# Low weight parts on GpSimd around hand-overs, and tiles that sweep the high weights first, in a two-layer streaming encoder

## What is computed

```python
def swiglu(x, w_gu, w_dn):
    gate, up = jnp.split(x @ w_gu, 2, axis=-1)
    return (jax.nn.silu(gate) * up) @ w_dn

def trunk_layer(...):
    x = x + 0.5 * rmsnorm(swiglu(rmsnorm(x, g[0]), w_gu0, w_dn0), g[1])
    u = rmsnorm(x, g[2])
    qa, ka, va, qb, kb, vb = jnp.split(u @ w_in, 6, axis=-1)
    ...
    mix = jnp.concatenate([oa, ob], axis=-1) @ w_out
    x = x + rmsnorm(mix, g[3])
    qc = rmsnorm(x, g[4]) @ w_cq
    oc = cross_attend(qc, mem_k, mem_v) @ w_co
    x = x + rmsnorm(oc, g[5])
    x = x + 0.5 * rmsnorm(swiglu(rmsnorm(x, g[6]), w_gu1, w_dn1), g[7])
```

## Time and profile before

| | |
|---|---|
| median of 3 runs | 2632.45 us (2627.0 to 2634.76) |
| the profiled execution's own time | 2635.67 us |
| its span, first to last instruction | 2633.9 us |
| PE busy | 2525.5 us, 96% |
| DVE, ACT, POOL busy | 1209.3, 912.3, 23.8 us |
| mean granted clock of PE | 0.982 |
| largest group of PE's waits | 19.7 us, for w_lo |

### The profile page before, as it was taken

The page is one execution under the profiler, slowest core; times in us unless marked ns, Lnnn a source line. Parts: engine busy times, 40 slices in busy tenths (PEclk is TensorE's granted clock), DMA queues, the critical chain, the costliest instruction groups (busy, mean ns, idle before and its releaser), DMA issues.

```text
span 2633.9 us, 47255 instructions
## 1 busy us (share of the span) xinstructions
PE 2525.5 (96%) x19325; PEld 2416.5 (92%) x19325; DVE 1209.3 (46%) x2059; ACT 912.3 (35%) x1650; POOL 23.8 (1%) x55
## 2 busy tenths in 40 slices
PE   6999999999999899999999999999999998999998
PEld 6999999997698799999989999989966988999998
DVE  4444325336747644442354442253466656444323
ACT  4222223225745522222232222242356545222221
POOL 1000000000000000000000000000000000000000
PEclk9999999999999999999999999999999998999999
DMA  6223333332123122232222223233411311322321
GB/s 185 87 85 89 95 88 102 98 114 91 39 83 105 36 85 88 88 99 81 77 64 88 88 88 99 85 97 115 125 55 49 115 47 50 94 87 84 94 87 66
DMA packets 384734, 229.81 MB, mean 87 GB/s; under 512 B 6892, under 2 KB 371454, under 8 KB 384608
## 3 DMA queue, kind: packets, MB, share of 16 engines
q1 hardware_dynamic: 379040, 206.66, 26.4%
q0 software_dynamic: 4368, 16.92, 1.9%
q10 hardware_dynamic: 1200, 4.46, 0.4%
HBM read 214.46 MB, written 18.79 MB: 89 GB/s over the span
## 4 chain that ended last, share of the span: by engine, by line
PE 88%; DVE 7%; ACT 2%; issue 1%; DMA 1%; DVEq 0%; ACTq 0%; SPq 0%
PE psum L671 75%; PE psum L646 4%; PE psum L959 3%; PE psum L727 2%; PE psum L991 2%; DVE w_lo L1495 1%; DVE x L1533 1%; PE psum L686 1%; ACT w_hi L1164 1%; DVE u_lo L1490 1%; PE psum L973 1%; DVE y_mix L1530 1%; DMA w_raw<-in_w_ffn_gu 0%; DMA w_raw<-in_w_cq 0%; DVE y_ffn L1530 0%
## 5 line engine op out<-in xcount | busy, mean ns | idle before, releaser
L671 PE MATMUL psum<-u_hi,w_hi 128*128 128x272 f32 x3840 | 815.8, 291 | 26.9 <-DVE w_lo L1495 19.7
L671 PE MATMUL psum<-u_hi,w_lo 128*128 128x272 f32 x3840 | 806.1, 289 | 0.0
L671 PE MATMUL psum<-u_lo,w_hi 128*128 128x272 f32 x3840 | 805.2, 288 | 0.0
L1164 ACT ACTIVATE w_hi<-w_raw 128x1024 fp32r<-128x1024 f32 (+1 forms) x336 | 376.6, 1121 | 1109.6 <-PE psum L671 1040.1
L671 PEld LDWEIGHTS psum<-u_hi,w_hi 128*128 128x128 f32 x3840 | 608.8, 189 | 32.9 <-DVE w_lo L1495 22.8
L671 PEld LDWEIGHTS psum<-u_lo,w_hi 128*128 128x128 f32 x3840 | 610.7, 189 | 0.0
L671 PEld LDWEIGHTS psum<-u_hi,w_lo 128*128 128x128 f32 x3840 | 606.4, 189 | 0.0
L1495 DVE TENSOR_TENSOR w_lo<-w_raw,w_hi 128x1024 fp32r<-128x1024 f32 (+1 forms) x336 | 436.3, 1299 | 317.4 <-ACT w_hi L1164 316.7
L671 PE MATMUL psum<-h_hi,w_hi 128*128 128x272 f32 x1408 | 307.5, 290 | 0.4
L671 PE MATMUL psum<-h_lo,w_hi 128*128 128x272 f32 x1408 | 304.8, 287 | 0.0
L671 PE MATMUL psum<-h_hi,w_lo 128*128 128x272 f32 x1408 | 304.6, 287 | 0.0
(11 more groups left out here) (242 smaller groups left out, 2220.2 us busy)
## 6 DMA issues: line engine op xcount, KB each, us to landing
w_raw<-in_w_ffn_gu SPq DMA_DIRECT2D x176, 512.0 KB, 3.7
w_raw<-in_w_ffn_dn SPq DMA_DIRECT2D x64, 704.0 KB, 4.4
w_raw<-in_w_in SPq DMA_DIRECT2D x48, 512.0 KB, 3.6
w_raw<-in_w_out SPq DMA_DIRECT2D x16, 512.0 KB, 3.5
w_raw<-in_w_ckv SPq DMA_DIRECT2D x16, 512.0 KB, 3.6
bias_tab_dram<-bias_rev_dram POOLq DMA_DIRECT2D x1, 5120.0 KB, 20.5
out<-k_nat POOLq DMA_DIRECT2D x4, 1024.0 KB, 5.0
out<-v_nat POOLq DMA_DIRECT2D x4, 1024.0 KB, 5.7
```

Of the source, the lines that this page charges most:

```text
L671: pe_last[0] = pe.matmul(psum[:, bank + part, 0:c1 - c0], w, xx[:, c0:c1], start=s0, stop=s1)
L1164: return act.activation(out, src, ACT.Copy, scale=scale)
```

## The change

`cut_lo` exists on Pool too. Pool takes the low cuts of the first two pairs of the projection, the last three of the attention output and the first of memory, the second query pair, both cross output pairs, and the first two pairs of each FFN that follows a hand-over. DVE keeps the others. Where the turn passes from one engine to the other, the first cut waits until `w_lo_ready` has the other's last count. `chunk` and `half_chunk` become `sweeps`: behind a wait for w_hi alone all blocks of the high weights, on the high and the low inputs, and behind a wait for w_lo the low weights. A `hook` is called before every third of its terms (a term is one weight block on one input, two matmuls or one for a half), so hook k stands k/8 of the way; some hooks are moved. `first_chunks` has a new order in both its forms. On DVE the cuts leave the hand-overs; `add_y` and `recip_y` of the second half stand between the low parts. On ACT six instead of four u_hi stand before the late piece of y behind an FFN, and the squares of half B before the next pair's cut. `product` and the loops that call it keep their order and their waits.

The hunks below are, in order: Pool's `cut_lo` and its calls; PE's `sweeps`, the body of `first_chunks`, the hooks of the last down tile and of the third projection tile; ACT's `late_half`; DVE's `late_sums`, its hooks at the end of an FFN, and the cuts that leave DVE in the output, query and cross-attention stages.

```diff
+        def cut_lo(pair, slot, behind_dve=False):
+            if behind_dve:
+                pool.wait_ge(w_lo_ready, 2 * pair + slot)
+            pool.wait_ge(w_hi_ready, 2 * pair + slot + 1)
+            pool.tensor_tensor(w_blocks(w_lo, slot, 8), w_blocks(w_raw, slot, 8),
+                               w_blocks(w_hi, slot, 8).bitcast(F32), ALU.subtract).then_inc(w_lo_ready, 1)
...
+            cut_pair(base + AT_IN, True)
+            cut_pair(base + AT_IN + 1)
             store_keys(l, 0, *k_outs[0])
...
             store_values(l, 1, *v_outs[1])
+            cut_pair(base + AT_OUT + 1, True)
+            for j in range(2, 5):
+                cut_pair(base + AT_OUT + j)
...
+            cut_pair(base + AT_CQ + 1, True)
+            cut_pair(base + AT_CO)
+            cut_pair(base + AT_CO + 1)
             pool.wait_ge(mem_stored, l * 32 + 32)
+            cut_pair(base + AT_FFN[1])
+            cut_pair(base + AT_FFN[1] + 1)
+            if l + 1 < DEPTH:
+                cut_pair(base + PAIRS, True)
+                cut_pair(base + PAIRS + 1)
...
+        def sweeps(pair, slot, bank, inputs, blocks, first, last, half=None, hook=None):
+            n = len(blocks)
+            pe.wait_ge(w_hi_ready, 2 * pair + slot + 1)
+            for i in range(2 * n):
+                if hook and i % 3 == 0:
+                    hook(i // 3)
+                b, low = divmod(i, 2)
+                term(w_hi, slot, b, bank, inputs(blocks[b])[low], first and i == 0, False, half)
             pe.wait_ge(w_lo_ready, 2 * pair + slot + 1)
+            for b in range(n):
+                if hook and (2 * n + b) % 3 == 0:
+                    hook((2 * n + b) // 3)
+                term(w_lo, slot, b, bank, inputs(blocks[b])[0], False, last and b == n - 1, half)
...
+            pe.wait_ge(w_hi_ready, 2 * pair + 1)
+            if norm_late:
+                sweep(0, 0, w_hi, 0, range(4))
+                pe.wait_ge(w_lo_ready, 2 * pair + 1)
+                sweep(0, 0, w_lo, 0, range(4))
+                norm_late()
+                sweep(0, 0, w_hi, 0, range(4, KD))
+                sweep(0, 0, w_lo, 0, range(4, KD))
+                spread_late()
+                sweep(0, 0, w_hi, 1, last=True)
+                pe.wait_ge(w_hi_ready, 2 * pair + 2)
+                sweep(1, 0, w_hi, 0)
+                sweep(1, 0, w_hi, 1)
+                pe.wait_ge(w_lo_ready, 2 * pair + 2)
+                sweep(1, 0, w_lo, 0, last=True)
+                for k in range(KD):
+                    for slot in range(2):
+                        one(slot, 1, w_hi, 0, k)
+                        one(slot, 1, w_lo, 0, k)
+                for slot in range(2):
+                    sweep(slot, 1, w_hi, 1, last=True).then_inc(chunk_done, 1)
+            else:
+                sweep(0, 0, w_hi, 0)
+                pe.wait_ge(w_lo_ready, 2 * pair + 1)
+                sweep(0, 0, w_lo, 0)
+                pe.wait_ge(w_hi_ready, 2 * pair + 2)
+                sweep(1, 0, w_hi, 0)
+                pe.wait_ge(w_lo_ready, 2 * pair + 2)
+                sweep(1, 0, w_lo, 0)
+                for slot in range(2):
+                    sweep(slot, 1, w_hi, 0)
+                    sweep(slot, 1, w_lo, 0)
+                for slot in range(2):
+                    for half in range(2):
+                        mm = sweep(slot, half, w_hi, 1, last=True)
+                    mm.then_inc(chunk_done, 1)
...
             def early(k):
-                if k == 4:
+                if k == 2:
                     norm_y(l, st, 0)
-                if k == 8:
+                if k == 5:
                     spread_y(l, st, 0)
...
             def norms(k):
-                if k == 3:
+                if k == 5:
                     norm_x(q, 4)
-                if k == 6:
+                if k == 7:
                     spread_x(q, 0, 4)
                     spread_x(q, 1, 5)
...
             for k in range(KD):
                 high(q, 1, k, gain)
-            cut_hi(pair + 1, 0)
             for p in range(4):
                 square_x(q, 1, p)
+            cut_hi(pair + 1, 0)
             cut_hi(pair + 1, 1)
...
-        def late_sums(q, pair):
-            fold_x(q, 0)
-            cut_lo(pair + 1, 0)
-            sum_x(q, 0)
-            fold_x(q, 1)
-            cut_lo(pair + 1, 1)
-            sum_x(q, 1)
+        def late_sums(q):
+            for half in range(2):
+                fold_x(q, half)
+                sum_x(q, half)
...
-            def between(p):
-                if p == 1 and more:
-                    cut_lo(after, 0)
-                if p == 2:
+            def later(k):
+                if k == 2:
                     add_y(l, st, 8)
-                if p == 3:
+                if k == 5:
                     recip_y(l, st, 1)
-            def later(k):
-                if k == 3:
-                    cut_lo(after, 1)
...
-                cut_lo(base + AT_OUT + m // 2 + 1, m % 2)
...
-            cut_lo(base + AT_CQ + 1, 0)
-            cut_lo(base + AT_CQ + 1, 1)
...
-            attention(l, CROSS, {7: lambda: cut_lo(base + AT_CQ + 2, 0), 10: lambda: cut_lo(base + AT_CQ + 2, 1)})
+            attention(l, CROSS)
...
-            cut_lo(crossed + 1, 0)
...
-            cut_lo(crossed + 1, 1)
...
-                if p == 1:
-                    cut_lo(crossed + 2, 0)
...
-                if k == 3:
-                    cut_lo(crossed + 2, 1)
```

More of the change, by code:

```diff
@@ L663, in product @@
             hi, lo = xs
[L664 to L680, removed]
+            term(w_hi, slot, b, bank, hi, start, False, half)
+            term(w_hi, slot, b, bank, lo, False, False, half)
@@ L682, in token_sums @@
+            term(w_lo, slot, b, bank, hi, False, stop, half)
         def token_sums(sums, half, bank, col):
@@ L731, in first_chunks @@
[L731 to L739, removed]
-            sweep(1, second, 0, w_lo, 0)
-            sweep(0, 0, 0, w_hi, 1, last=True)
-            sweep(1, second, 0, w_hi, 1, last=True)
@@ L744, in first_chunks, with one @@
-            sweep(0, 0, 1, w_hi, 0, first=True)
-            sweep(0, 0, 1, w_lo, 0)
-            sweep(1, second, 1, w_hi, 0, first=True)
-            sweep(0, 0, 1, w_hi, 1, last=True).then_inc(chunk_done, 1)
-            sweep(1, second, 1, w_lo, 0)
-            sweep(1, second, 1, w_hi, 1, last=True).then_inc(chunk_done, 1)
+            fresh = {(slot, half) for slot in range(2) for half in range(2)}
+            def one(slot, half, weight, part, k, last=False):
+                u = (u_hi, u_lo)[part]
+                pe.wait_ge((u_hi_ready, u_lo_ready)[part], 16 * q + 8 * half + k + 1)
+                mm = pe.matmul(psum[:, (0, second)[slot] + half, 0:H], weight[:, slot, k * 128:(k + 1) * 128],
+                               u[:, k, half * H:half * H + H], start=(slot, half) in fresh, stop=last and k == KD - 1)
+                fresh.discard((slot, half))
+                return mm
@@ new lines, in sweep @@
+            def sweep(slot, half, weight, part, ks=range(KD), last=False):
+                for k in ks:
+                    mm = one(slot, half, weight, part, k, last)
+                return mm
+            pe.wait_ge(w_hi_ready, 2 * pair + 1)
[13 more added lines that the diff above has]
+                sweep(1, 0, w_lo, 0, last=True)
+                for k in range(KD):
+                    for slot in range(2):
[18 more added lines that the diff above has]
+                    mm.then_inc(chunk_done, 1)
@@ L1537, in update_half @@
                 dve.wait_ge(x_ready, 8 * q + 4 * half + 4)
[L1538 removed]
+            for k in range(KD):
+                if gain is not None:
                     low(q, half, k, gain)
[L1540 to L1541 removed]
+                if later:
+                    later(k)
         def fold_x(q, half):
```

106 lines of the change are left out of this document (50 added, 56 removed).

## The result

The changed kernel takes 2646.22 us (median of 5 runs, 2645.07 to 2647.91) against 2632.45 of the kernel before (5 runs, 2627.0 to 2635.31). The ratio (of the means) is 1.0056, with a 95% interval of 1.0041 to 1.0071: it is slower, by more than the 0.3% that a measurement of this kernel can tell from no change. The prediction said 2612 and gave this side a chance of 0.10; its range ended at 2632.

What follows compares the result with a forecast made beforehand. PE, busy 96%, bounds the kernel through hand-over gaps and slow-clock matmuls behind them. Terms 8.0 + 16.6 + 6.8 + 7.6 - 2.2 = 36.8 us saved, 4.2 if held; middle 20.5 from 2632.45 gives 2612.0, range 2590 to 2632.

Steps and rivals of the forecast that it cites:

- The bound above: Whole kernel: every DVE operation on two SBUF tiles waits out Pool's cut; 4.2 us saved, against 36.8 with no hold.
- The middle: Whole kernel: Pool's cuts hold DVE partly; 20.5 us saved, 2612.0 us, own range 2601 to 2622, chance 0.42.
- The rival: DVE held for the whole cut, Pool's next-pair cuts falling on the sums chain: 4.2 us saved, 2628, chance 0.20.
- Query projection, twice: nothing: PE done 2 us sooner but sumx comes as now: nothing saved; under the full hold -3.5 us each.
- FFN to projection: 6.8 saved at the third tile: Half B starts 3.0 us earlier, third tile at 451.0 not 457.78; 8.3 each with the fourth, 2.5 under hold.
- one of the signs named for wrong: DVE's low parts of half B ending no earlier; others were sumx as PE's largest wait, Pool cuts above 3.7 us.
- the sums, with no cuts between them, end about 453.3: FFN to projection: norm asked for at 454.7, so the 2.03 us sumx wait goes; third to fourth tile 1.5 less.
- Cross-attention output to FFN: Two cuts leave DVE's chain: 3.8 us saved each, 7.6 for two; under the full hold -1.5 each.
- FFN to FFN: The one hand-over between FFNs: same earlier start as FFN to projection, 6.8 us saved; 3.4 under the full hold.
- The certain part: Tiles start on high weights only: 6.4 at FFN starts, 1.1 in last down tiles, 0.5 first hand-over; 8.0 us saved.
- attention and output projection: Output projection's third tile pays Pool's longer cut in full: 1.1 us lost each, 2.2 for two.
- The cut is too long for the output projection: Slower rival: Pool cuts of 5 us make output projections, cross-attention outputs and hand-overs wait for w_lo; 2653 us, chance 0.08.

Runs made afterwards that it cites:

- Experiment 9: The changed kernel with forty idle matmuls put in PE's wait ahead of the norm of x in the query projection: 2644.57 us, ratio 1.0056.
- the run with fills: The changed kernel with Pool filling w_lo with zeros in place of the subtraction, so low weights of its pairs are wrong: 2597.97 us, one run.
- experiment 11: run 6 with the query projection's norm of x asked for behind 12 matmuls of the third tile: 2602.4 us, ratio 0.9892.
- experiment 10: The changed kernel with the norm of x asked for inside the third query tile, behind 30 matmuls, Pool's cuts kept: 2638.65 us, ratio 1.0026.
- run 6: The changed kernel with Pool cutting only the first pair behind an FFN, DVE the second pairs behind the sums of x: 2610.59 us, ratio 0.9917.

## Why the prediction was wrong

**The failed step is the choice between the bounds of the unknown cost.** The bound above, "each DVE operation on two SBUF tiles waits out the cut", is what happens. The middle was argued with half of the update's operations reading PSUM (true: 0.71, untouched) and with low parts being mostly not waited for. But the cuts of the second pairs fall on the sums, where every instruction reads two SBUF tiles, and PE waits for the sums. The rival named just that place and got 0.20.

**And the full hold was priced too low:** it gave 4.2 saved where 13.8 were lost (10.8 by the traces). The prediction took 1.6 us a cut (2.3 less an operation of 0.72); the held sum and fold lose 2.0 and 2.1, nearly a whole cut each, because they run behind the cut and not inside it (2.48 for a sum of 0.44). Two terms show it; how the prediction came from 1.6 to its figures by stage it did not write out.

- *"Query projection, twice: nothing"*, and -3.5 each under the hold; measured +7.7 and +5.1. In the first layer PE's norm starts 829.17 - 823.25 = 5.9 later, of which 1.3 came in with it and 0.5 was lost between the update and the sums: 4.2 of hold (2.0 and 2.1), where I had 3.5. From the norm to the eviction it then takes 8.1 us in place of 5.1: 3.1 of low clock, which stood nowhere in my sum, though its first paragraph had said that a hand-over costs twice. Experiment 9 takes those 3 us away by itself. Even with nothing held the step was wrong: "PE would be done 2 us sooner" only to wait means 2.49 us idle in the run with fills, a clock of 0.50 behind it, and 4.4 us lost in two layers.
- *"FFN to projection: 6.8 saved at the third tile"* came in good part: the tile starts at 453.20, 4.6 sooner than in the earlier trace rows. It did not come by the predicted way, half B 3.0 earlier: half B's update starts 13.1 us after half A's, where it was 12.8 before and 10.7 with fills, and half B's low parts end at 448.15 + 3.39 = 451.54 against 451.68, which is one of the signs named for wrong. What differs is PE: 45 matmuls at a clock of 1.00 from 450 to 456 where there were 31 at 0.56, and 16 matmuls behind the last u_lo. In the other direction, "the sums, with no cuts between them, end about 453.3" fell: the sum of half A took 2.53 and the fold of half B 3.45, the last sum ends at 460.68, PE waits 3.49 for it, and the clock is 0.65 over the next 9 us (42 matmuls against 59). From -2.5 under my hold it became +1.3 each. Cross-attention output to FFN went the same way: +3.6 and +0.8, +2.2 on average, where I had +1.5 under the hold. The held sum of squares and low part, 4.1 us for 2.4 of cuts, stood in no term.

**What held.** With the hold taken away, the sum of the terms does come out: -37.8 us with fills, -36.8 predicted; at FFN to projection 15.7 of 16.6, at FFN to FFN 6.5 of 6.8. Cross-attention was better than its term and the query projection worse, fills are also shorter than the 2.3 us of the sum, and part of the 12.8 at cross-attention is a low clock in the second layer of the kernel before's own trace (4.9 in the first layer, 7.9 in the second), so the agreement is partly luck. The certain part was right (9.1 of 8.0), though not its 0.5 in the program's first hand-over, for which it named no row: that stretch takes 54.89 us, 54.77 before. So was the price of a cut on Pool: 2.3 taken, 2.39 alone and 2.54 on average. The output projection's third tile waits 4.02 us, with 3.9 given. That attention and output projection lost 2.1 of 2.2 is a sum of 0.3 and 1.8, while the wait grew by 1.2 in each layer, so that agreement is luck:

```profile
739.63 0.52 PE L698 MATMUL psum<-u_hi,w_hi 128*128 128x272 f32 x2 [4.02 <-POOL w_lo L623]
```

The Trainium skill (GPSIMD Engine Reference, Elementwise — side-by-side cycle accounting), from which the prediction had the estimate 2.25 us, comes near: measured are 2.39 and 2.54. *The cut is too long for the output projection* needed cuts above 3.7 us and did not decide.

## What to carry to other kernels

Before moving an elementwise instruction from VectorE to GpSimd, list what VectorE runs beside it: with two SBUF operands on both, one waits for the other's end, and two cuts in a row catch a back-to-back chain twice. Add up what is held against what is taken away: here 1.5 us for two cuts of 1.22 behind an FFN gained, 4.1 for the same two behind cross-attention lost. Where PE waits for VectorE's next results, putting the instruction later on VectorE itself, behind them, gained where Pool lost. And count a PE wait that grows as two terms, the wait and the slow matmuls behind it; if work can be put over it, the second can go as well, if little of the wait is left (it went with 0.98 us left in experiment 11, and not with 2.97 in experiment 10).

## What was not expected of the hardware

The hold works in both directions: Pool's cut of 2.39 us takes 2.90 when it meets DVE's additions. This is the cut alone, POOL in the kernel after:

```profile
755.75 2.39 POOL L623 TENSOR_TENSOR w_lo<-w_raw,w_hi 128x1024 fp32r<-128x1024 f32 x1 [3.11 <-ACT w_hi L1211]
```

Behind PE's waits for the sums of the first query projection, the clock stayed at 1.00 after 0.72 us (before), 1.37 (run 6) and 1.77 (run 9). It fell after 2.49 (fills; 0.50 from 816 to 822), 2.97 (run 10) and 6.67 (after). The norm itself, 12 matmuls of one column, takes 1.50 us before and in run 9, and 2.60 with fills and 2.63 in run 10.

For shorter waits the length alone does not decide. In the second layer of the kernel before the wait at this place is 0.73 us, as in the first, and yet the clock over the 8 us behind it is 0.79; in the changed kernel it is 0.79 behind the 1.24 us at cross-attention to FFN. A short wait was no guarantee of the full clock; what else it hangs on is not shown here.
